# Combining the experts: the addition to x moved from VectorE to GpSimd, with two update buffers

## The reference

```python
x = x + gate2 * rms_norm(ffn(h), g_post2)
# rms_norm(x, g) = x * rsqrt(mean(x * x) + EPS) * g
# ffn of the second layer: for each token the two best of 8 experts, weighted by their shares
```

## Time and profile before

| what | value |
|---|---|
| runs of the kernel before | 2096.12, 2094.29, 2095.29 us; median 2095.29 us |
| span of the profiled execution, first to last instruction | 2094.4 us |
| median less that span (what lies around it) | 0.9 us |
| PE busy over the span | 1937.5 us (93%) |
| DVE busy | 1296.8 us (62%) |
| ACT busy | 1045.6 us (50%) |
| POOL busy | 93.0 us (4%), 62 instructions |

### The profile page before, as it was taken

How to read it: one execution, slowest core, us unless ns; L and a number is a source line. 1 busy time by engine, 2 the same in 40 slices (tenths; PEclk the granted TensorE clock), 3 DMA queues, 4 the chain that set the end, 5 groups by cost and what they waited for, 6 DMA issues and landing times. The chain is left out here.

```text
span 2094.4 us, 31993 instructions
## 1 busy us (share of the span) xinstructions
PE 1937.5 (93%) x11352; PEld 1620.5 (77%) x11352; DVE 1296.8 (62%) x1958; ACT 1045.6 (50%) x1689; POOL 93.0 (4%) x62
## 2 busy tenths in 40 slices
PE   4998899899999999997998999987999999999993
PEld 2996555599999998986986555876888888888883
DVE  4725656574323323266627565656888888888886
ACT  4214344454112111144234344546888888888884
POOL 0320000000000000001300000001000000000001
PEclk9999999899999999998999999898999999999997
DMA  6205512202223213203125601158957191826464
GB/s 253 95 26 201 199 41 101 101 1 81 70 77 106 71 61 91 81 31 115 47 81 214 267 1 41 62 211 351 410 221 305 66 355 51 335 105 266 177 243 160
DMA packets 130340, 302.25 MB, mean 144 GB/s; under 512 B 17985, under 2 KB 63937, under 8 KB 127297
## 3 DMA queue, kind: packets, MB, share of 16 engines
q1 hardware_dynamic: 124240, 279.10, 36.5%
q10 hardware_dynamic: 3120, 11.28, 1.4%
q0 software_dynamic: 2880, 10.49, 1.3%
HBM read 358.73 MB, written 28.61 MB: 185 GB/s over the span
## 5 line engine op out<-in xcount | busy, mean ns | idle before, releaser
L2278 DVE TENSOR_TENSOR ex_wl<-ex_raw,ex_wh 128x1024 fp32r<-128x1024 f32 x351 | 419.9, 1222 | 26.9 <-ACT ex_wh L2156 17.3
L2156 ACT ACTIVATE ex_wh<-ex_raw 128x1024 fp32r<-128x1024 f32 x351 | 368.1, 1060 | 73.5 <-PE psum L2213 48.3
L2557 PE MATMUL psum<-norm_out,ex_w_hi 128*128 128x320 f32 x1408 | 268.8, 309 | 2.7 <-PEq L1586 2.7
L2213 PE MATMUL psum<-ex_wh,ex_he_hi 128*128 128x512 f32 (+1 forms) x624 | 243.1, 390 | 14.0 <-DVE ex_wl L2278 14.0
L2213 PE MATMUL psum<-ex_wl,ex_he_hi 128*128 128x512 f32 (+1 forms) x624 | 233.6, 374 | 0.0
L2213 PE MATMUL psum<-ex_wh,ex_he_lo 128*128 128x512 f32 (+1 forms) x624 | 233.0, 373 | 0.0
L2557 PEld LDWEIGHTS psum<-norm_out,ex_w_hi 128*128 128x128 f32 x1408 | 223.4, 189 | 3.0 <-DVE ex_w_lo L2428 2.8
L2428 DVE TENSOR_TENSOR ex_w_lo<-side,ex_w_hi 128x1024 fp32r<-128x1024 f32 (+1 forms) x82 | 82.7, 1014 | 166.1 <-ACT ex_w_hi L2424 165.7
L2557 PE MATMUL psum<-norm_out,ex_w_lo 128*128 128x320 f32 x704 | 165.9, 309 | 0.0
L2213 PEld LDWEIGHTS psum<-ex_wh,ex_he_hi 128*128 128x128 f32 x624 | 118.1, 189 | 36.1 <-issue 17.1
L2213 PEld LDWEIGHTS psum<-ex_wh,ex_he_lo 128*128 128x128 f32 x624 | 118.4, 190 | 22.2 <-issue 2.9
(11 more groups left out here) (406 smaller groups left out, 3821.0 us busy)
## 6 DMA issues: line engine op xcount, KB each, us to landing
ex_raw<-moe_gate_up SPq DMA_DIRECT2D x221, 512.0 KB
ex_raw<-moe_w_down SPq DMA_DIRECT2D x143, 512.0 KB
x<-moe_gate_up SPq DMA_DIRECT2D x65, 512.0 KB
wmod_ssd<-w_mod SPq DMA_DIRECT2D x56, 512.0 KB, 5.9
wmod_at<-w_mod SPq DMA_DIRECT2D x24, 512.0 KB, 4.2
side<-ffn_w_gate SPq DMA_DIRECT2D x22, 512.0 KB, 3.9
side<-ffn_w_up SPq DMA_DIRECT2D x22, 512.0 KB, 3.9
mx_qkv_room<-w_in SPq DMA_DIRECT2D x10, 1024.0 KB, 4.9
```

Source lines behind the costliest of these rows:

```text
L2156: act.activation(wh[:, i % RING], raw_of(i), ACT.Copy).then_inc(*hi_done.up(1))
L2213: last = pe.matmul(p.psum[:, 2 + g % 2, 0:width], h[:, k], w[:, i % RING, cols], start=(k == 0 and m == 0), stop=(k == KD - 1 and m == 2))
L2278: dve.tensor_tensor(wl[:, i % RING], raw_of(i), wh[:, i % RING].bitcast(F32), ALU.subtract).then_inc(*lo_done.up(1))
L2557: last = pe.matmul(p.psum[:, home[i] + half, 0:HT], m[:, i % w.RING, cols], x[:, k, half * HT:(half + 1) * HT], start=(k == 0 and n == 0), ...
```

## The change

The addition `x + upd` of each block goes from VectorE's list to GpSimd's, behind the ten indirect DMAs. A new signal `upd_ready` is raised by the update and waited for by the addition. VectorE no longer waits for its own update through `dve_chain`, and from block 2 on it waits, before the reciprocal of block b, until the addition of block b - 2 is done, since it will write the same half of `upd`. The signal `res`, for which SyncE waits before it stores a block, is now raised by GpSimd.

```diff
@@ stage_combine
     shared, mixed, x_back, eps_set = p.sig("co_shared"), p.sig("co_mixed"), p.sig("co_x_back"), p.sig("co_eps")
+    upd_ready = p.sig("co_upd_ready")
@@ GpSimd
                             ).then_inc(*fetched[b].up(16))
+                pool.wait_ge(*x_back.at(0))
+                for b in range(TB):
+                    pool.wait_ge(*upd_ready.at(b + 1))
+                    pool.tensor_tensor(p.x[:, b], p.x[:, b], upd[:, b % 2], ALU.add).then_inc(*res.up())
@@ VectorE
                 blend(0)
-                dve.wait_ge(*x_back.at(0))
                 for b in range(TB):
                     if b + 1 < TB:
                         blend(b + 1)
+                    if b >= 2:
+                        dve.wait_ge(*res.at(b - 1))
                     dve.wait_ge(*r2.at(b + 1))
                     link(dve, dve.reciprocal(rstd2[:, b:b + 1], rstd2[:, b:b + 1]))
-                    link(dve, dve.scalar_tensor_tensor(out=upd[:, b % 2], in0=got[:, b, 0], scalar=rstd2[:, b:b + 1],
-                                                       in1=rows[:, SEQ_OF[b]], op0=ALU.mult, op1=ALU.mult))
-                    dve.tensor_tensor(p.x[:, b], p.x[:, b], upd[:, b % 2], ALU.add).then_inc(*res.up())
+                    dve.scalar_tensor_tensor(out=upd[:, b % 2], in0=got[:, b, 0], scalar=rstd2[:, b:b + 1],
+                                             in1=rows[:, SEQ_OF[b]], op0=ALU.mult, op1=ALU.mult).then_inc(*upd_ready.up())
```

## The result

| | median us | runs | lowest and highest |
|---|---|---|---|
| before | 2095.61 | 10 | 2093.64, 2097.59 |
| changed | 2099.82 | 10 | 2098.49, 2101.74 |

The ratio is 1.0022, with a 95% interval of 1.0013 to 1.0030: 4.2 us slower. The span of the profiled execution is 2097.1 us, and its own time was 2098.82, so 1.7 us lie around the span.

The account below looks back on a forecast made before the run. VectorE alone was taken to bound the last 15 us; with additions on GpSimd holding it, the steps sum to 20.0 us against 15.46, so 2095.29 + 4.5, rounded up to 2100.0 us, range 2097.8 to 2102.2.

Parts of the forecast that it names:

- addition 0 and blend 2: From the first update's end: GpSimd starts 0.08 us behind, holds VectorE 2.14, and the blend of block 2 takes 1.28.
- addition 4: Last block's addition, on a free GpSimd before the store: starts 0.08 us behind and takes 2.38, so 2.46.
- The exclusion: A GpSimd addition and VectorE's blends or updates, which read two SBUF tiles, don't share: one stands still, 2.14 us an addition.
- first rival: No exclusion between blend or update and addition: GpSimd becomes the bound, 2.3 us better, 2093.0 us; chance 0.06.
- Its size: VectorE's loss beside GpSimd in the input projection's convolution, 2.09 ns an element: 2.14 us per addition instead of 1.23.
- second rival: Each GpSimd addition excludes VectorE for its whole instruction, with handovers: +5.5 to +6.3 us, 2101.3 us; chance 0.16.
- third rival: GpSimd starts late behind its indirect DMAs; beyond 3.9 us counts in full, at 6 us late 2102.0 us; chance 0.06.
- The buffer wait: VectorE's new wait for the addition of block b - 2, before the reciprocal: costed at nothing; three buffers would move nothing.
- Level at the start: Addition 0 and blend 2 become ready together after the first update; whichever is first, the other queues.
- What lies around the span: The median lies 0.9 us above the profiled span of 2094.4 us, which becomes 2098.9.
- The chances: Slower by over about 0.2% (4.2 us, beyond 2099.5) 0.68, within 0.2% 0.30, faster 0.02; main case 0.72.

Follow-up runs that it names:

- the kernel without the exclusion: Changed kernel with one input of both update and blend read from PSUM: stretch 12.48 us, median 2091.41 us, ratio 0.9981 to the kernel before.
- the one with two halves: Changed kernel with each GpSimd addition cut into two of 128x512: stretch 19.21 us, median 2099.41 us, ratio 1.0024 to the kernel before.

## Why the prediction was right

It forecast 2100.0 us, and the median is 2099.82; +4.5 for the stretch, and it measured +4.40. The mechanism was the one forecast, and the closeness of the numbers is in part luck, as said below. Term by term, in the profile of the changed kernel:

| step | predicted us | measured us |
|---|---|---|
| addition 0 and blend 2 | 2.22 + 1.28 = 3.50 | 2077.76 - 2074.18 = 3.58 |
| reciprocal 1, update 1 | 1.38 | 1.39 |
| blend 3 | 1.20 | 1.20 |
| addition 1, update 2 | 3.42 | 3.28 |
| blend 4 | 1.20 | 1.20 |
| addition 2, update 3 | 3.42 | 3.28 |
| addition 3, update 4 | 3.42 | 3.50 |
| addition 4 | 2.46 | 2.42 |
| sum | 20.0 | 19.85 |

- **The exclusion** is the mechanism, and it is shown: with one input of each instruction of VectorE moved to PSUM it goes away, with PSUM and no GpSimd nothing changes, and a fill, which reads nothing, doesn't cause it. The first rival (no exclusion here) falls. What it forecast, 2.3 us less than before, is near what the kernel without the exclusion shows: 3.0 us less.
- **Its size.** 2.14 us per addition was read off a convolution with other shapes. It is 2.11 when the addition comes first. When the addition has queued, the update stands 1.89 us, and with the reciprocal's 0.10 that hides under it VectorE is held 2.0. So this term was 0.14 too large twice, and 0.08 too small twice (3.58 for 3.50, 3.50 for 3.42): the errors partly cancel.
- **The rule of the whole instruction** (second rival, +5.5 and more) falls: VectorE goes on some 0.2 us before the end that GpSimd's record shows, taking an update's own work as the 1.28 us that it lasts alone. The update that began at 2080.46 worked from 2083.63 - 1.28 = 2082.35, and the addition ended at 2082.56.
- **The late start** (third rival): the first addition began at 2074.34, 0.16 us behind the update's end, where 0.08 was taken. But GpSimd had been idle for 0.92 us by then, and for 0.88 us or more in every run here. A start cost of up to that would be hidden, and no run shows GpSimd go from an indirect DMA straight to arithmetic. One of 6 us is excluded.
- **The buffer wait** at nothing: right, by the run with three buffers. It binds where GpSimd falls behind, as in the run with the update from PSUM and in the one with two halves.
- **Level at the start:** "whichever is first, the other queues" was right for the exclusion and wrong for the sum. The order is worth 0.5 us, the blend first being the better. The profiled execution of the changed kernel had the worse one, which the sum happened to assume; in the profiles of the eight variants with additions, a copy or a fill on GpSimd the blend was first. With it the stretch would have been some 19.4 us, and the forecast of 20.0 would have been 0.6 too high. How the ten runs divide isn't in the trace.
- **What lies around the span** was taken as 0.9 us, the median less the profiled span. It is 1.7 in this run (2098.82 - 2097.1), and 1.7 to 1.8 in every run on record with both numbers. It did no harm, since the forecast was the median plus a difference; with 1.7 around its span the execution profiled before took some 2096.1, above the median of 2095.29, by my estimate.
- The chances put 0.68 on slower by over 0.2%. The ratio is 0.22% above 1 (0.20% by the two medians), so it came out so by a hair, and the interval holds both sides of that bound.

## What to carry to other kernels

Before work moves from VectorE to GpSimd, ask what both read: if GpSimd's instruction reads SBUF and VectorE's neighbours read two SBUF tiles each, they took turns in every trace here, and GpSimd's slower pace was simply added (here 2.0 to 2.1 us for an addition of 1.23). Look for a stretch of the same trace where the two already overlap; the price can be read there. Where the offload is wanted, put one input of VectorE's instructions in PSUM: here it turned 4.4 us lost in the stretch into 3.0 us gained.

## What the runs showed of the hardware that was not expected

- A GpSimd copy that reads one tile excludes VectorE's two-tile instructions as well (update 2.07 us in place of 1.28), while a fill that writes the same tile does not (1.28).
- The profile counts a VectorE instruction that stands still as busy, and puts the waiting of a GpSimd instruction into its duration too (3.32 for 2.34): no row names the engine for which it stood.
- GpSimd's addition of 128x1024 took 2.34 us by itself, 0.05 below the line through its 128 and its 2048 elements, which gave 2.39.
- GpSimd's indirect DMAs wait for a blend that reads two SBUF tiles (up to 1.99 us in place of 0.94) and don't hold it up in turn (1.28 us).
